# Expert blocks' token rows picked on chip by one-hot products instead of stored to memory and gathered

## Chip, cores and metric

One core of one Trainium2 chip runs the whole kernel in one launch. The metric is the device time of that launch in microseconds; lower is better.

## What is computed

Two stacks of layers follow each other on 256 latent tokens of width 1024 (256 context tokens take part in the first mixer only). The first stack has two layers, each a mixer (latent attention, then a short convolution) and a hierarchical mixture of experts. The second stack has two layers of feed-forward, attention with retention, and feed-forward again. The change touches the two mixtures of experts alone:

```
g_sel  = argmax(softmax(h @ w_group) + b_group)          # 1 of 4 groups
e_prob = softmax(logits of the 8 experts of that group)
top_w, expert_id = the 2 best of them, weights normalised, times the group's probability
for each token and each of its 2 experts e:
    y += top_w * ((silu(x @ w_gate[e]) * (x @ w_up[e])) @ w_down[e])
```

There are 32 experts of three matrices of 1024 x 512 floats (2 MB each). Everything is f32.

## The kernel before, in words

The class Moe holds an expert stage; it is used twice. `pe`, `act`, `dve` and `pool` write the program of each engine by hand, and semaphores tie them together; the order on every engine's queue is the order of the code. Tokens lie features first: A and XT hold 8 tiles of 128 features by 512 tokens. After the first mixer the context half of XT (columns 256 to 511) is not read again.

**Start of a stage.** TensorE computes the router's logits (L1495), turns the normalised tokens into rows (L1503), and runs filler products (L344, `keep_busy`). VectorE selects the experts in a long row of short steps. TensorE counts, with a triangular matrix, each token's rank within its expert (L1511). An expert's tokens are cut into blocks of CAP = 32; VectorE derives block (BLK, L1803) and place within the block (RANK) of each of the two choices of each token. One-hot matrices of place and block, multiplied (L1525), give a table that has for each block and place the token's number and weight. Meanwhile ScalarE copies the token rows out of PSUM (L1633) and stores them to the DRAM tensor f_rows (L1636). When the store has landed and the table is kept (L1821), POOL gathers the 32 rows of block 0 into XG by an indirect DMA (L1874).

**A block.** In a loop over experts, and within it over the expert's blocks (bounds read from FIRSTI):

- TensorE: gate and up products (L1573, four column groups of the array side by side), then `turn_block` (L1545: eight transposes of the gathered rows of the next block into bank 3), `combine` of the previous block's result (L1538), transposes of the hidden rows (L1589), down products (L1598).
- ScalarE: Silu (L1661), `keep_tokens` (L1652, bank 3 to XB), copy of the result (L1667), and the load of the down matrix two experts ahead (L1676).
- VectorE: Silu times up (L1833), copies of the turned hidden rows (L1839), COMBINE, the matrix that scatters the block's rows back to their tokens (L1843).
- POOL: the gather two blocks ahead (L1880, L1874).
- SP: gate and up matrices four experts ahead (L3002), issued when the expert's last L1573 is done. Ten matrices are loaded ahead of the stage: slots of the ring, three slots in the arena and A.

SP's loop of loads begins after table_kept. The lines of the change are L1393 to L1411 (semaphores), L1447 to L1460 (tiles), L1522 to L1558 and L1576 to L1578 (TensorE), L1628 to L1655 and L1663 (ScalarE), L1805 to L1843 (VectorE), L1861 to L1900 (POOL) and L2990 (SP).

## Time and profile before

| | |
|---|---|
| runs | 2455.12, 2461.4, 2458.9 us, median 2458.9 |
| span of the profiled execution | 2451.3 us |
| TensorE busy | 2077.8 us (85%), weight loads 1590.7 (65%) |
| VectorE, ScalarE, POOL busy | 1134.3 (46%), 796.4 (32%), 109.6 us (4%) |
| bytes moved | 668.86 MB, mean 273 GB/s; queue q0 (gathers) 4.20 MB |
| blocks (executions of L1833) | 70: 36 in the first expert stage, 34 in the second |

No time of the profiled execution outside of its span is shown; the span stands 7.6 us below the median of the runs, and holds all the work between the first and the last instruction. In the timeline a row is start, duration, engine, line, operation, output <- input, shapes, count, and in brackets the idle time before and what ended it. In a view by windows the columns are the stretch and its length, then busy us and instruction count of TensorE products, TensorE weight loads, VectorE, ScalarE and POOL, then the mean granted TensorE clock (1.00 is 2.4 GHz, 0.50 is 1.2 GHz), the DMA engines' busy share, and GB/s. A group of instructions has its busy time and the mean ns of one, then the idle time before them and what ended it.

### The profile page before, as it was taken

The numbers are of one execution on the slowest core, as the hardware profiler recorded it, in microseconds if no ns is written. First come the engines' busy times: TensorE is split into PE (matmuls) and PEld (weight loads), VectorE is DVE, ScalarE is ACT, GpSimd is POOL, SyncE is SP. The second block draws the span as 40 slices with busy tenths as digits, with TensorE's granted clock in tenths as the row PEclk, the third lists the DMA queues.
The fourth block names the chain that finished last, engine by engine and source line by source line (L and its number), as shares of the span: only waits on it lengthen the run. The fifth ranks groups of instructions, "written<-read, shape, count | busy, mean of one in ns | idle before, by whom it ended". The sixth has DMA issues, their size and how long they took to land.

```text
span 2451.3 us, 46085 instructions
## 1 busy us (share of the span) xinstructions
PE 2077.8 (85%) x17112; PEld 1590.7 (65%) x17113; DVE 1134.3 (46%) x2111; ACT 796.4 (32%) x1534; POOL 109.6 (4%) x188
## 2 busy tenths in 40 slices
PE   7999778666768988655557999998999999998997
PEld 3567455434446955433334788886888788886886
DVE  4677211111115641111111666776666766867666
ACT  2233101000004420000000554554554554554554
POOL 0000100000000000000000000000000000000001
PEclk9999888888879988988888999999999999999999
DMA  9875899999997569999998755325546456334552
GB/s 391 325 287 190 329 414 421 414 424 429 419 376 282 192 257 409 424 428 421 422 422 360 274 185 171 137 93 172 172 153 209 153 160 193 132 117 142 173 157 83
DMA packets 277458, 668.86 MB, mean 273 GB/s; under 512 B 8656, under 2 KB 203216, under 8 KB 252240
## 3 DMA queue, kind: packets, MB, share of 16 engines
q1 hardware_dynamic: 264416, 532.99, 57.9%
q10 hardware_dynamic: 9360, 129.96, 12.6%
q0 software_dynamic: 3552, 4.20, 0.5%
q8 instruction: 78, 1.28, 0.2%
q14 instruction: 52, 0.43, 0.1%
HBM read 669.48 MB, written 3.15 MB: 274 GB/s over the span
## 4 chain that ended last, share of the span: by engine, by line
PE 70%; DMA 14%; another core or an unknown queue 6%; DVE 5%; issue 3%; ACT 2%; SPq 1%; POOL 0%; POOLq 0%; ACTq 0%; DVEq 0%; PEldq 0%
PE ps L2180 19%; PE ps L2185 10%; PE ps L1573 9%; DMA A<-in_moe_w_up 6%; PE ps L1598 4%; DMA ring<-in_moe_w_up 4%; PE ps L2454 4%; DMA arena<-f_rows,arena 3%; PE ps L1538 2%; PE ps L1545 2%; PE ps L2619 2%; PE ps L1983 1%; PE ps L1985 1%; PE ps L1984 1%
## 5 line engine op out<-in xcount | busy, mean ns | idle before, releaser
L2180 PE MATMUL ps<-XS,WS 128*128 128x512 f32 x1408 | 499.7, 399 | 8.9 <-DVE XS L689 7.8
L2165 DVE TENSOR_TENSOR WS<-ring,WS 128x1024 fp32r<-128x1024 f32 (+1 forms) x276 | 329.5, 1195 | 226.2 <-ACT WS L2160 225.8
L2185 PE MATMUL ps<-XS,WS 128*128 128x256 f32 x1408 | 396.7, 282 | 0.0
L2160 ACT CAST WS<-ring 128x1024 fp32r<-128x1024 f32 (+1 forms) x276 | 283.0, 1026 | 328.3 <-PE ps L2185 315.0
L1833 DVE TENSOR_TENSOR arena<-arena,ps 64x256 f32<-64x256 f32 x70 | 29.6, 424 | 706.8 <-ACT arena L1661 706.8
L2180 PEld LDWEIGHTS ps<-XS,WS 128*128 128x128 f32 x1408 | 265.4, 188 | 79.3 <-DVE XS L689 18.5
L2185 PEld LDWEIGHTS ps<-XS,WS 128*128 128x128 f32 x1408 | 268.0, 190 | 0.2 <-issue 0.2
L1573 PE MATMUL ps<-arena 128*32 128x256 f32 x1632 | 159.1, 460 | 109.4 <-DMA arena<-in_moe_w_up 74.3
L1573 PE MATMUL ps<-ring,arena 128*32 128x256 f32 x2240 | 160.6, 450 | 101.3 <-DMA ring<-in_moe_w_up 93.4
L2180 PE MATMUL ps<-HS,WS 128*128 128x512 f32 x616 | 216.4, 396 | 0.0
L1598 PE MATMUL ps<-ring,arena 128*32 128x256 f32 x2240 | 165.3, 445 | 54.8 <-DVE arena L1839 54.8
L1573 PEld LDWEIGHTS ps<-ring,arena 128*32 128x32 f32 x2240 | 94.6, 129 | 168.7 <-issue 146.8
L1573 PEld LDWEIGHTS ps<-arena 128*32 128x32 f32 x1632 | 90.5, 132 | 174.5 <-issue 151.8
L2185 PE MATMUL ps<-HS,WS 128*128 128x256 f32 x704 | 197.7, 281 | 0.0
L1661 ACT ACTIVATE arena<-ps 64x256 f32<-64x256 f32 x70 | 26.3, 376 | 501.0 <-PE ps L1573 501.0
L1598 PEld LDWEIGHTS ps<-ring,arena 128*32 128x32 f32 x2240 | 88.6, 125 | 102.3 <-issue 84.0
L2185 PEld LDWEIGHTS ps<-HS,WS 128*128 128x128 f32 x704 | 133.4, 189 | 0.1
L2180 PEld LDWEIGHTS ps<-HS,WS 128*128 128x128 f32 x616 | 115.5, 188 | 26.8
L1667 ACT COPY arena<-ps 128x256 f32<-128x256 f32 x70 | 26.1, 372 | 290.8 <-PE ps L1598 290.8
L1545 PEld LDWEIGHTS ps<-BASE,arena 32*128 32x128 f32 x576 | 68.7, 198 | 56.7 <-issue 51.3
L2454 PE MATMUL ps<-XS,WS 128*128 128x256 f32 x768 | 100.4, 288 | 0.0
L1839 DVE COPY arena<-ps 64x128 f32<-64x128 f32 x140 | 39.7, 284 | 129.2 <-PE ps L1589 127.0
(352 smaller groups left out, 3212.4 us busy)
## 6 DMA issues: line engine op xcount, KB each, us to landing
ring<-in_moe_w_down ACTq DMA_DIRECT2D x60, 2048.0 KB, 14.4
ring<-in_ffn_w_gu SPq DMA_DIRECT2D x90, 1024.0 KB, 7.3
ring<-in_moe_w_gate SPq DMA_DIRECT2D x32, 2048.0 KB, 44.3
ring<-in_moe_w_up SPq DMA_DIRECT2D x32, 2048.0 KB, 52.4
arena<-in_moe_w_gate SPq DMA_DIRECT2D x32, 2048.0 KB, 44.3
ring<-in_w_mod SPq DMA_DIRECT2D x24, 2048.0 KB, 11.7
ring<-in_ffn_w_down SPq DMA_DIRECT2D x32, 1408.0 KB, 6.4
arena<-in_moe_w_up SPq DMA_DIRECT2D x16, 2048.0 KB, 53.0
```

Source lines behind the costliest of these rows:

```text
L1538: mm = pe.matmul(self.combined_tile(2 * q + i), self.YS[rows, i * P:(i + 1) * P], self.COMBINE[rows, :], start=False, stop=last and i == 1)
L1545: mm = pe.transpose(ps[:, 3, c * CAP:(c + 1) * CAP], by_eight[:, c, :], IDENT[0:CAP, 0:CAP])
L1573: mm = pe.matmul(ps[self.lane_rows(q), 0, 0:HALF_FF], x, weight, start=k == 0, stop=k == KD - 1)
L1598: mm = pe.matmul(ps[self.lane_rows(q), 7, 0:D // 4], self.HB[:, c, :], down[:, c, q * (D // 4):(q + 1) * (D // 4)], start=c == 0, stop=c = ...
L1833: v.tensor_tensor(self.H[0:2 * CAP], self.SG[2 * CAP:P], ps[2 * CAP:P, 0, 0:HALF_FF], ALU.mult)\
L1839: v.tensor_copy(self.HB[h * 2 * CAP:(h + 1) * 2 * CAP], turned[:, h]).then_inc(self.h_kept.sem, 1)
L2160: L.inc(L.eng.copy(self.parts(u)[0], source), self.w_high)
L2165: L.inc(L.eng.tensor_tensor(wl, self.unit(u)[1], high(wh), ALU.subtract), self.w_split)
L2180: L.eng.matmul(ps[:, bank, :].rearrange("p (j t) -> p j t", j=2), wh[:, i, :], moving[:, :, k, :], start=k == 0, stop=False)
L2185: mm = L.eng.matmul(ps[:, bank, 0:TL], wl[:, i, :], moving[:, 0, k, :], start=False, stop=k == total - 1)
L2454: mm = pe.matmul(out_ap, weights[:, k, :], XS[:, x, k, :], start=k == 0 and x == 0 and weights is high_part, stop=k == KD - 1 and weights ...
L2619: mm = pe.matmul(self.y_tile(m), weights[:, k - first, cols], YS[:, k, x, :], start=m % 2 == 0 and k == 0 and x == 0 and weights is high_part,
```

## The change

The rows stay on chip: ScalarE copies them into the context half of XT (ROWS). The store, f_rows, the gathers, XG, the index table and the turns of the gathered rows go. VectorE makes for each block a one-hot matrix PICK of 128 tokens by 32 places for each of the two token tiles (match: is AT, the token's block times 32 plus place less 32 for each block gone by, equal to 0..31; pick_matched adds the two choices; shift takes 32 off). TensorE multiplies with the rows as the stationary operand and PICK as the moving one (pick_block): 8 column tiles by 2 token tiles, accumulated, which gives the block's tokens features first, as the turns did. The first pick_block now stands before the zero products and the table; the table moves from bank 6 to bank 7, the fillers behind the zero products go, and the block loops and SP wait for `ranges` (FIRSTI) instead of the table.

```diff
-                self.rows_out = [shared(f"moe_rows_out{i}", 16 * NT // 2) for i in range(2)]
-                self.block_turned = sig(f"moe{l}_block_turned")
+                self.picks = sig(f"moe{l}_picks")
+                self.matched = sig(f"moe{l}_matched")
+                self.shifted = sig(f"moe{l}_shifted")
+                self.picked = sig(f"moe{l}_picked")
...
-                self.XG = take(D)
+                self.AT = take(2 * NT)
+                self.MATCH = take(2 * NT * CAP).rearrange("p (c t a) -> p c t a", c=2, t=NT)
+                self.PICK = take(NT * CAP).rearrange("p (t a) -> p t a", t=NT)
...
-                self.ROWS = [arena[:, rows_at + i * D:rows_at + (i + 1) * D] for i in range(2)]
+                self.ROWS = [XT[:, 4 * t:4 * t + 4, TL:TA] for t in range(NT)]
...
+                def pick_block():
+
+                    for c in range(KD):
+                        for t in range(NT):
+                            mm = pe.matmul(ps[:, 3, c * CAP:(c + 1) * CAP], self.ROWS[t][:, c // 2, c % 2 * P:(c % 2 + 1) * P],
+                                           self.PICK[:, t, :], start=t == 0, stop=t == NT - 1)
+                    mm.then_inc(self.picked.sem, 1)
+
+                zeros = self.YS.bitcast(BF16)
+                L.wait(self.rows_kept, NT)
+                pe.wait_ge(self.picks.sem, 1)
+                pick_block()
+                pe.wait_ge(self.y_kept.sem, 1)
+                for bank in (1, 4, 5, 6):
+                    pe.matmul(ps[:, bank, :], zeros[:, 0:P], zeros[:, 0:512], start=True, stop=False)
...
-                def turn_block():
-                    for c in range(KD):
-                        mm = pe.transpose(ps[:, 3, c * CAP:(c + 1) * CAP], by_eight[:, c, :], IDENT[0:CAP, 0:CAP])
-                    mm.then_inc(self.block_turned.sem, 1)
...
-                keep_busy(L, 7, 7)
-                pe.wait_ge(self.gathered.sem, 16)
-                turn_block()
...
-                        pe.wait_ge(self.gathered.sem, b * 16 + 32)
+                        pe.wait_ge(self.picks.sem, b + 2)
                         pe.sem_inc(spare.sem, 1)
-                        turn_block()
+                        pick_block()
...
-                    L.inc(act.copy(self.ROWS[t % 2], ps[:, 1 + 2 * (t % 2):3 + 2 * (t % 2), :].rearrange("p b n -> p (b n)")),
-                          self.rows_kept)
-                    L.join()
-                    act.dma_start(f_rows[t * P:(t + 1) * P, :], self.ROWS[t % 2]).then_inc(self.rows_out[t % 2].sem, 16)
+                    for q in range(4):
+                        rows = ps[:, 1 + 2 * t:3 + 2 * t, :].rearrange("p b n -> p (b n)").rearrange("p (n c) -> p c n", c=KD)
+                        L.inc(act.copy(self.ROWS[t][:, q, :].rearrange("p (i n) -> p i n", i=2), rows[:, 2 * q:2 * q + 2, :]),
+                              self.rows_kept if q == 3 else None)
...
+                step(v.scalar_tensor_tensor(out=self.AT, in0=self.BLK, scalar=float(CAP), in1=self.RANK, op0=ALU.mult, op1=ALU.add))
+
+                def match():
+
+                    return v.tensor_tensor(self.MATCH.rearrange("p c t a -> p (c t) a"),
+                                           IOTA[:, 0:CAP].unsqueeze(1).to_broadcast([P, 2 * NT, CAP]),
+                                           self.AT.unsqueeze(2).to_broadcast([P, 2 * NT, CAP]), ALU.is_equal)
+
+                def shift():
+                    return v.tensor_scalar(self.AT, self.AT, -float(CAP), None, ALU.add)
+
+                def pick_matched():
+                    return v.tensor_tensor(self.PICK, self.MATCH[:, 0], self.MATCH[:, 1], ALU.add)
+
+                step(match())
+                pick_matched().then_inc(self.picks.sem, 1)
+                L.inc(shift())
+                L.inc(v.tensor_copy(self.FIRSTI, self.FIRST), self.ranges)
...
+                        v.wait_ge(self.shifted.sem, b + 1)
+                        match().then_inc(self.matched.sem, 1)
+                        v.wait_ge(self.picked.sem, b + 2)
+                        v.sem_inc(spare.sem, 1)
+                        v.wait_ge(self.matched.sem, b + 1)
+                        pick_matched().then_inc(self.picks.sem, 1)
+                        shift().then_inc(self.shifted.sem, 1)
...
-                g.memset(self.XG, 0.0).then_inc(self.index_g.sem, 1)
                 g.memset(self.COMBINE, 0.0).then_inc(self.combine_made.sem, 1)
-                L.wait(self.table_kept, 1)
...
-                sp.wait_ge(moe.table_kept.sem, moe.table_kept.base + 1)
+                sp.wait_ge(moe.ranges.sem, moe.ranges.base + 1)
```

## Rows read from the trace of the kernel before

**Rows 1.** The page, section 2: GB/s moved in 40 slices of the span.

```profile
GB/s 391 325 287 190 329 414 421 414 424 429 419 376 282 192 257 409 424 428 421 422 422 360 274 185 171 137 93 172 172 153 209 153 160 193 132 117 142 173 157 83
```

**Rows 2.** View by windows: engine busy us (instructions), mean PEclk, DMA share, GB/s.

```profile
285.00:760.00 475.00, 346.21 (x4416) 217.82 (x4416) 61.32 (x189) 46.13 (x118) 39.67 (x71) 0.84 0.97 402
900.00:1360.00 460.00, 303.05 (x4232) 197.09 (x4232) 54.33 (x172) 38.48 (x104) 38.56 (x69) 0.86 0.98 406
```

**Rows 3.** Groups of instructions by line, 240 to 760 us, TensorE's first products of a block.

```profile
L1573 PE MATMUL ps<-ring,arena 128*32 128x256 f32 x1152 | 89.1, 477 | 48.9 <-DMA ring<-in_moe_w_up 45.0 <-issue 3.8
```

**Rows 4.** Timeline, TensorE, one block at full clock and the next's start.

```profile
402.78 3.66 PE L1573 MATMUL ps<-ring,arena 128*32 128x256 f32 x64 [0.24 <-issue]
406.37 0.96 PE L1545 MATMUL ps<-BASE,arena 32*128 32x32 f32 x7
407.06 0.49 PE L1538 MATMUL ps<-arena 32*128 32x256 f32 x3
...
409.55 1.93 PE L1598 MATMUL ps<-ring,arena 128*32 128x256 f32 x32 [0.78 <-DVE arena L1839]
412.36 3.66 PE L1573 MATMUL ps<-ring,arena 128*32 128x256 f32 x64 [0.87 <-issue]
```

**Rows 5.** Timeline, TensorE, first L1573 and last L1598 of both expert stages.

```profile
275.74 5.48 PE L1573 MATMUL ps<-ring,arena 128*32 128x256 f32 x64 [1.60 <-issue]
...
748.31 1.93 PE L1598 MATMUL ps<-ring,arena 128*32 128x256 f32 x32 [0.78 <-DVE arena L1839]
...
900.50 3.66 PE L1573 MATMUL ps<-ring,arena 128*32 128x256 f32 x64 [0.90 <-ACT arena L1652]
...
1355.64 1.93 PE L1598 MATMUL ps<-ring,arena 128*32 128x256 f32 x32 [0.78 <-DVE arena L1839]
```

**Rows 6.** View by windows, stretches at half clock.

```profile
286.30:289.60 3.30, 3.30 (x32) 1.89 (x36) 0.46 (x2) 0.00 (x0) 0.08 (x1) 0.50 0.04 11
296.60:299.90 3.30, 3.30 (x36) 1.97 (x34) 0.36 (x1) 0.00 (x0) 0.00 (x0) 0.50 0.98 420
887.00:890.40 3.40, 3.40 (x11) 2.22 (x11) 2.47 (x14) 0.00 (x0) 0.00 (x0) 0.50 0.29 116
890.50:893.80 3.30, 3.30 (x6) 1.60 (x6) 1.09 (x2) 0.00 (x0) 2.19 (x3) 0.50 0.00 0
```

**Rows 7.** Timeline, 289 to 300.5 us, two blocks without a weight wait between.

```profile
289.64 3.69 PE L1573 MATMUL ps<-ring,arena 128*32 128x256 f32 x64
...
293.55 0.35 SPq L3002 DMA_DIRECT2D ring<-in_moe_w_gate  x1
...
296.45 3.61 PE L1598 MATMUL ps<-ring,arena 128*32 128x256 f32 x32 [0.78 <-DVE arena L1839]
...
299.76 3.77 PE L1573 MATMUL ps<-ring,arena 128*32 128x256 f32 x64
```

**Rows 8.** View by windows, a stretch with a gather and one without.

```profile
520.00:530.00 10.00, 5.33 (x76) 2.93 (x72) 0.00 (x0) 0.37 (x1) 0.00 (x0) 0.83 1.01 403
540.00:550.00 10.00, 8.41 (x96) 5.09 (x97) 1.14 (x4) 0.75 (x2) 1.04 (x2) 0.71 1.01 433
```

**Rows 9.** Timeline, POOL, the gather before the first of these stretches.

```profile
518.44 0.93 POOL L1874 DMA_INDIRECT arena<-f_rows,arena  x1 [0.85 <-POOL arena L1880]
```

**Rows 10.** Groups by line and form: 879 to 883 us, and 239.5 to 243.2 us.

```profile
L1511 PE MATMUL ps<-arena,BASE 128*128 128x32 f32 x6 | 1.5, 405 | 2.3 <-DVE arena L1763 2.3
...
L1495 PE MATMUL ps<-VECS,A 128*128 128x36 f32 x32 | 3.7, 277 | 0.0
```

**Rows 11.** Timeline, VectorE and TensorE at the start of the expert stages.

```profile
256.98 0.16 DVE L1803 TENSOR_TENSOR arena<-arena 128x4 f32<-128x4 f32 x1
257.18 0.29 DVE L1810 TENSOR_SCALAR arena<-BASE,arena 128x128 f32<-128x128 f32 x1
...
886.88 2.62 PE L1525 MATMUL ps<-arena 128*128 128x98 f32 x8 [0.60 <-DVE arena L1815]
...
889.29 1.92 PE L1555 MATMUL ps<-arena 128*128 128x512 bf16 x4
```

More of the change, by code:

```diff
@@ L252, in carver @@
             return take
-        f_rows = nc.dram_tensor("f_rows", [TL, D], F32, kind="Internal").ap()
         const_in = sig("const_in")
@@ L1569, in expert @@
                         for k in range(KD):
-                            x = self.XB[:, k, :]
+                            x = self.XB[:, k * CAP:(k + 1) * CAP]
                             for q in range(4):
@@ L1600, in expert @@
                         mm.then_inc(self.down.sem, 1)
+                L.wait(self.ranges, 1)
                 with pe.Fori(0, EXPERTS // AHEAD) as turn:
@@ L1645, in act @@
                 L.inc(act.activation(self.ES, self.ES, ACT.Exp), self.exps)
-                for t in range(2, NT):
-                    store_rows(t)
                 load_table(L, ACT.Silu)
-                L.wait(self.table_kept, 1)
                 def keep_tokens():
-                    act.copy(self.XB.rearrange("p c a -> p (c a)"), ps[:, 3, 0:8 * CAP]).then_inc(self.x_kept.sem, 1)
-                act.wait_ge(self.block_turned.sem, 1)
+                    act.copy(self.XB, ps[:, 3, 0:KD * CAP]).then_inc(self.x_kept.sem, 1)
+                act.wait_ge(self.picked.sem, 1)
                 keep_tokens()
+                L.wait(self.ranges, 1)
                 def expert(turn, a):
@@ L1688, in act @@
                     self.next_norm.act_square(L, k)
-                L.wait(self.gathered_all, 1)
                 end(L, "act")
@@ L1816, in dve @@
                                               PLACE[:, 2, t:t + 1], ALU.is_equal, ALU.mult), self.places)
-                step(v.tensor_copy(self.FIRSTI, self.FIRST))
-                L.wait(self.table, 1)
-                tab = ps[:, 6, 0:2 * NB].rearrange("p (c b) -> p c b", c=2)
-                step(v.tensor_scalar(self.EMPTY, tab[:, 1, :], 0.5, OUT_OF_BOUNDS, ALU.is_lt, ALU.mult))
-                step(v.scalar_tensor_tensor(out=self.TABI, in0=tab[:, 1, :], scalar=-1.0, in1=self.EMPTY, op0=ALU.add, op1=ALU.add),
-                     self.table_kept)
-                step(v.tensor_copy(self.TAB, tab), self.table_kept)
                 for t in range(NT):
@@ L1826, in dve @@
                 L.join()
+                step(match())
+                v.wait_ge(self.picked.sem, 1)
+                pick_matched().then_inc(self.picks.sem, 1)
+                shift().then_inc(self.shifted.sem, 1)
+                L.wait(self.table, 1)
+                tab = ps[:, 7, 0:2 * NB].rearrange("p (c b) -> p c b", c=2)
+                step(v.tensor_copy(self.TAB, tab), self.table_kept)
                 def expert(turn, a):
@@ L1866, in pool @@
                 g.memset(self.YS, 0.0).then_inc(self.y_kept.sem, 1)
-                for i in range(2):
-                    L.wait(self.rows_out[i], 16 * (NT // 2))
-                g.memset(self.XG, 0.0).then_inc(self.index_g.sem, 1)
                 g.memset(self.COMBINE, 0.0).then_inc(self.combine_made.sem, 1)
-                L.wait(self.table_kept, 1)
-                def load_rows(indices):
-                    g.indirect_dma_start(out=self.XG[0:CAP], out_offset=None, in_=f_rows,
-                                         in_offset=bass.IndirectOffsetOnAxis(ap=indices, axis=0),
-                                         bounds_check=self.T - 1, oob_is_err=False).then_inc(self.gathered.sem, 16)
-                def gather(block, indices):
-                    g.tensor_copy(self.IDXG[0:CAP], self.TABI[0:CAP, block]).then_inc(self.index_g.sem, 1)
-                    g.wait_ge(self.index_g.sem, indices + 1)
-                    g.sem_inc(spare.sem, 1)
-                    load_rows(self.IDXG[0:CAP])
-                g.wait_ge(self.index_g.sem, 1)
-                load_rows(self.TABI[0:CAP, 0:1])
-                blocks = self.count_of(g)
-                g.wait_ge(self.gathered.sem, 16)
-                g.wait_ge(self.block_turned.sem, 1)
-                gather(slice(1, 2), 1)
-                with g.Fori(0, blocks) as b:
-                    g.wait_ge(self.gathered.sem, b * 16 + 32)
-                    g.wait_ge(self.block_turned.sem, b + 2)
-                    g.sem_inc(spare.sem, 1)
-                    gather(bass.ds(b + 2, 1), b + 2)
-                g.wait_ge(self.gathered.sem, blocks * 16 + 32)
-                g.sem_inc(self.gathered_all.sem, 1)
         take = carver()
```

31 lines of the change are left out of this document (8 added, 23 removed).

## The prediction, made before the changed kernel ran

> **What bounds the kernel now.** The page comes first. Its row of bytes moved, 40 slices of 61.3 us, shows where memory takes over: from about 310 to 670 us and from about 920 to 1290 us the DMA engines move 409 to 429 GB/s [rows 1]. These are the two expert stages, which stream 192 weight matrices of 2 MB once each. The view by windows confirms it: DMA share 0.97 to 0.98 over each stage while TensorE is busy 346 of 475 us and 303 of 460 us [rows 2]. The view of groups by line, cut to the first stage, says what TensorE waits for: 45.0 us for the expert weights in the ring slots alone to land ahead of L1573, in a group that holds a little over half of its matmuls [rows 3]. So the weight stream sets the pace in steady state, and TensorE has slack. How much slack is the question, since the change takes work from DMA and gives work to TensorE.
>
> The timeline of one undisturbed block answers that [rows 4]. L1573 starts at 402.78, the eight turns of L1545 at 406.37, the combination L1538 at 407.06, the turns of the hidden rows (L1589) follow, L1598 starts at 409.55 and lasts 1.93, and the next L1573 starts at 412.36: 9.58 us a block. There are 36 blocks in the first stage and 34 in the second (one L1833 each, counted in the table above) for 32 experts each. The first stage's blocks run from 275.74 to 748.31 + 1.93 = 750.24, the second's from 900.50 to 1355.64 + 1.93 = 1357.57 [rows 5]. That is 474.5 and 457.1 us, so 13.2 and 13.4 us a block: 3.6 to 3.9 us above 9.58 at full clock.
>
> Not all of this is waiting. Between the end of L1573 and the start of L1598, TensorE does only thin work for 3.2 us: turns of 32 rows, a combination with 32 rows, a pause of 0.78 us for VectorE. In blocks that follow each other without a weight wait, the granted clock is then 0.50, level 1.2 GHz, right behind this thin stretch (286.3 to 289.6, 296.6 to 299.9) [rows 6]. L1598 takes 3.61 instead of 1.93 us, but the next L1573 starts at once, where after a fast L1598 it starts 0.87 us late; the period is 299.76 - 289.64 = 10.12 us [rows 7].
>
> **The change, part by part.**
>
> *Removed from DMA.* Two stores of 512 KB and a gather for each block in each stage. Gathers cost more than their bytes: the stretch from 520 to 530 us runs at 403 GB/s, the one from 540 to 550 us at 433 [rows 8]; the first holds the rows of the gather issued at 518.44 [rows 9]. Half of such stretches at 7% less is 3.5% of 440 us, some 15 us a stage, if the weights stay the bound. It is worth nothing if TensorE becomes the bound, and I find below that it does.
>
> *Removed from TensorE.* Eight turns a block; the next group starts 407.06 - 406.37 = 0.69 us after them [rows 4]. The fillers of L344 at the start go too.
>
> *Added to TensorE.* pick_block: 8 column groups times 2 token tiles are 16 products. L1511 is the same form (128x128 stationary, 32 moving, f32): 3 products show as 6 instructions, so 32 instructions a block. At full clock 32 of L1495, with 36 moving columns, fill 3.7 us with a mean of 277 ns, so they start (3.7 - 0.28) / 31 = 0.11 us apart: 3.5 us. At half clock six of L1511 take 1.5 us with a mean of 405 ns, (1.5 - 0.405) / 5 = 0.22 apart: 7.0 us [rows 10]. The time is that of loading 128 columns to stream 32. No cover: it stands between L1573 and L1538, and TensorE works in order. VectorE's and ScalarE's part (Silu, product) needs 0.8 us there and was already covered.
>
> The block at full clock is therefore 9.58 - 0.69 + 3.5 = 12.4 us, 36 of them 446 us.
>
> *What the clock does to it.* The thin stretch grows from 3.2 to 3.2 - 0.69 + 3.5 = 6.0 us. Is pick_block work of the kind behind which the clock falls, or of the kind of L1573, behind which it is back? From 887.0 to 890.4 TensorE is busy without a gap (3.40 of 3.40 us), most of it with L1525: products with a 128x128 stationary operand whose loads take most of the time, as pick_block's are. The clock is 0.50 there and still 0.50 from 890.5 to 893.8 [rows 6]. TensorE had no gap and the clock did not rise. So I put pick_block with the thin work. One fall a block costs what rows 7 show: L1598 +1.7, the re-issue gap -1.07 (0.87, and 0.20 of overlap), sum 12.4 + 0.6 = 13.1 us (the same arithmetic gives 10.2 before, 10.12 seen). A stretch that is nearly twice as long holds a second fall, of some 3.3 us like those shown: it lies on pick_block or the next L1573 and costs half of itself, less what falls on the pause: 1.3 us, so 14.4 us. I take two falls in three blocks of five, 13.9 us. Below, nothing falls: 12.4. Above, all at half clock: 6.8 + 7.0 + 2 + 1.3 + 3.6 = 20.7 us, which I take as far off, since L1573 brought full clock back each time [rows 6, 7].
>
> The Trainium skill, page "TensorE: Matmul & The Clock Gate", section "HAM oscillation — how this bites in real kernels", gives as its rule that the clock is lost to idle gaps of TensorE, above all to waits for DMA. By that rule the change, which puts work where no gap is and shortens the weight waits, would keep the clock up: a block of 12.4 us and the time of rival B. The stretch from 887.0 to 890.4 [rows 6] has no gap and speaks against it.
>
> *Is the weight stream then still in the way?* An expert's 6.29 MB at 433 GB/s [rows 8] are 14.5 us; 36 blocks of 13.9 us over 32 experts are 15.6 us an expert, 34 blocks 14.8. TensorE is slower in both, so the weight waits go, and the gain on DMA with them.
>
> *Added to VectorE.* Three operations a block (128, 64 and 4 elements a lane), 0.29 us for the 128 (L1810 is such a comparison), 0.16 for the 4 (L1803), something between for the 64 [rows 11]: 0.7 us in all. They stand behind COMBINE, in a loop in which VectorE waits most of the block for ScalarE. Picks for the block after next are ready some 2 us after L1589; TensorE asks for them at the end of the next L1573, over 5 us later. Nothing. Uncovered they would cost 0.7 us a block. ScalarE: eight copies of 256 elements a lane in place of two of 1024, the same elements with six more starts, against two DMA issues and their waits removed, under VectorE's selection steps. Nothing; uncovered, an estimated 1 us a stage.
>
> *The start of a stage.* Before: store, wait for it, gather, turn, L1573 at 275.74 and 900.50 [rows 5]. After: from L1803 come AT, match and pick, three more VectorE steps, ready some 1.0 us after L1803 starts: at 258.0, and in the second stage at about 886.9, when L1525 started before [rows 11]. The clock is 0.50 there in the second stage [rows 6], and I take it so in the first, where the same short steps precede. pick_block 7.0, four zero products 1.7 (L1555, 1.92 with its tail), the table 2.6 (L1525): 11.3 to 11.4 us [rows 11]. L1573 starts at 269.4 and 898.3, that is 6.3 and 2.2 us earlier. The removed L344 fillers held the clock up in the second stage; its first L1573 will now run at half clock, +1.7. SP waited for table_kept and now waits for ranges, which comes earlier, then for the first expert's L1573; POOL is left with two memsets. On the queues of SP, ScalarE and POOL nothing new waits; VectorE has new waits on picked, with only pick_matched and shift behind them in the block.
>
> *Sum.* First stage: 269.4 + 36 x 13.9 + 1.7 = 771.5 against 750.2, +21.3. Second: 898.3 + 34 x 13.9 + 1.7 = 1372.6 against 1357.6, +15.0. Together +36.3 us on a profiled span of 2451.3. The median of the three runs is 2458.9, 7.6 above this span; added there: 2495 us.
>
> **Rivals.**
>
> *A, one fall a block (13.1 us).* Ends at 742.7 and 1345.4: -7.5 and -12.2, so 2439. For it: before, one fall is all that rows 6 show. Against: the stretch is twice as long. My 13.9 is a mixture of this and the next; the side changes at 13.4 us a block (36 x 13.4 + 34 x 13.4 + 3.4 - 8.5 = 933 against 931.6).
>
> *B, the clock holds (12.4 us): faster, and bound by weights.* The weights then end the stage: 86 loads of 2.10 MB after the ten that were prefetched, at 433 GB/s [rows 8], take 417 us. SP issues the first of them when expert 0's last L1573 is done, before at 293.55 [rows 7], then near 287 in the first stage (expert 0 has two blocks there) and 904 in the second. They end near 705 and 1322, and a block of 12.4 later the stages end at 718 and 1334: -32 and -23, so 2404. For it: TensorE has fewer gaps than before, and a product is no turn. Against: 887.0 to 893.8 [rows 6].
>
> *C, two falls in every block or more (14.4 us and up).* 36 x 14.4 + 34 x 14.4 give +39 and +32: 2530; every further 1 us a block adds 70. For it: the thin stretch is nearly twice as long in every block. Against: L1573 brought the clock back each time.
>
> **How the numbers follow.** Forecast (13.3 to 14.3 us a block) 0.60, A 0.12, B 0.15, C 0.13. The range reaches from A to a little beyond C, 2438 to 2535, and leaves out B and 0.05 of C. This kernel's measurement tells about 0.3% from no change, 7.4 us. Slower by more: the forecast but for 0.06 at its lower edge, and C: 0.67. Within: 0.09, that edge and 0.03 of A, blocks of 13.3 to 13.5 us. Faster: B and the rest of A: 0.24.
>
> **What would show it.** L1573 no longer waits for DMA after the first experts. The block period is near 13.9 us. Mean PEclk in the stages falls from 0.84 and 0.86 [rows 2] to 0.7 or lower. 32 pick instructions fill 3.5 us at full clock and 7.0 at half. DMA share falls below 0.95, with q0 gone. L1573 first starts near 269 and 898. I am wrong if the clock stays at 1.00 through pick_block, or if the stages still show 420 GB/s and more.

## The result, and the profile of the changed kernel

The changed kernel takes 2519.7 us in the median of four runs (2517.3 to 2525.6). The kernel before, run beside it on the same chip, takes 2457.0 (four runs, 2454.8 to 2461.4). The ratio is 1.025, 95% interval 1.023 to 1.028: slower by 63 us. The forecast was 2495 with a range of 2438 to 2535, so side and range hold, but the loss is nearly twice the 36 us of the sum.

The page of the changed kernel, three lines of section 2 (the span in 40 slices) and the first of section 4 (the chain that ended last):

```profile
PEclk9999777877778977787777799999999999999999
DMA  9975896999976558999997565534356456424542
GB/s 392 351 268 222 353 431 249 427 431 431 390 285 263 196 221 347 406 432 431 431 432 299 181 219 153 181 118 151 134 170 196 164 171 188 151 75 151 194 144 91
...
PE 89%; DVE 5%; issue 2%; ACT 1%; DMA 1%; SPq 0%; DVEq 0%; ACTq 0%; PEldq 0%
```

Section 3 no longer lists queue q0, the gathers'. Some slices still show 431 and 432 GB/s, the best of the stream, and others fall to 249 or 285, where before nearly all stood at 414 to 429 [rows 1]: the stream is faster when it runs, and runs less of the time. PEclk shows 7 and 8 all through the expert stages. The chain has DMA for 1%.

The view by windows, over the same two stretches as [rows 2]:

```profile
285.00:760.00 475.00, 445.67 (x4898) 306.83 (x4897) 68.57 (x264) 36.94 (x99) 0.00 (x0) 0.76 0.90 379
900.00:1360.00 460.00, 430.69 (x4535) 298.21 (x4537) 80.54 (x331) 43.31 (x112) 0.56 (x2) 0.75 0.93 393
```

TensorE is busy 445.7 and 430.7 us, where it was 346.2 and 303.1, at a clock of 0.76 and 0.75 where it was 0.84 and 0.86. The DMA share fell from 0.97 and 0.98 to 0.90 and 0.93. No wait of TensorE for a DMA is left in the first stage's L1565, where L1573 waited 45.0 us before [rows 3]. TensorE now ends both stages.

One block in TensorE's timeline (L1565 gate and up, L1520 the picks, L1547 the combination, L1581 the turns of the hidden rows, L1590 down), of the kind that fills the stages:

```profile
363.39 4.22 PE L1565 MATMUL ps<-arena 128*32 128x256 f32 x64
367.54 3.76 PE L1520 MATMUL ps<-arena,XT 128*128 128x32 f32 x32
371.23 1.99 PE L1547 MATMUL ps<-arena 32*128 32x256 f32 x16
373.15 0.64 PE L1581 MATMUL ps<-BASE,arena 64*64 64x64 f32 x4
374.57 3.64 PE L1590 MATMUL ps<-ring,arena 128*32 128x256 f32 x32 [0.78 <-DVE arena L1845]
377.95 0.53 PE L1565 MATMUL ps<-arena 128*32 128x256 f32 x2
```

The period is 377.95 - 363.39 = 14.56 us, against 9.58 in [rows 4]. The picks take 3.76. The combination takes 1.99 us where [rows 4] leaves it 1.3, and down takes 3.64, its time at half clock [rows 7], where the block of [rows 4] has 1.93. The granted clock of the stretches around it:

```profile
357.70:364.50 6.80, 6.02 (x60) 3.07 (x56) 1.66 (x7) 0.37 (x1) 0.00 (x0) 0.50 1.00 429
364.60:371.30 6.70, 6.70 (x92) 5.36 (x84) 0.42 (x1) 0.38 (x1) 0.00 (x0) 1.00 1.01 433
371.40:378.10 6.70, 5.92 (x56) 3.27 (x60) 1.66 (x7) 0.31 (x1) 0.00 (x0) 0.50 1.00 430
378.30:384.90 6.60, 6.60 (x93) 5.14 (x86) 0.42 (x1) 0.72 (x2) 0.00 (x0) 1.00 1.02 437
```

The picks and all but the first us of gate and up run at level 2.4 GHz. Behind the picks the clock is at 1.2 GHz through combination, turns, the pause and down, 6.7 us without a break, and comes back during the next gate and up. The fall does not stand at the same place in every block: in 41 of the 70 the picks take 3.7 us as here, in 29 they take 3.8 to 4.4, so that a part of them runs at the lower level. Of the 36 downs of the first stage 34 run at the lower level in whole or in part, of the 34 of the second 33; before it was 13 and 6.

Where the 68.0 us between the two profiled spans (2519.3 - 2451.3) lie, from the first and last rows of the stages in the timeline:

```profile
254.33 7.01 PE L1520 MATMUL ps<-arena,XT 128*128 128x32 f32 x32 [0.71 <-DVE arena L1804]
...
264.63 1.72 PE L1565 MATMUL ps<-ring,arena 128*32 128x256 f32 x20
...
777.80 3.48 PE L1590 MATMUL ps<-ring,arena 128*32 128x256 f32 x32 [0.78 <-DVE arena L1845]
...
931.30 1.93 PE L1565 MATMUL ps<-ring,arena 128*32 128x256 f32 x32
...
1417.77 3.64 PE L1590 MATMUL ps<-ring,arena 128*32 128x256 f32 x32 [0.78 <-DVE arena L1845]
```

| part | before [rows 5] | changed | difference | forecast |
|---|---|---|---|---|
| up to the first stage's first block | 275.74 | 264.63 | -11.1 | -6.3 |
| first stage, 36 blocks | 474.5 | 781.28 - 264.63 = 516.65 | +42.1 | 771.5 - 269.4 - 474.5 = +27.6 |
| between the stages | 150.3 | 931.30 - 781.28 = 150.0 | -0.2 | -2.2 |
| second stage, 34 blocks | 457.1 | 1421.41 - 931.30 = 490.1 | +33.0 | 1372.6 - 898.3 - 457.1 = +17.2 |
| behind it | 1093.7 | 1097.9 | +4.2 | 0 |

The blocks took 14.35 and 14.41 us on average, forecast 13.9. The 4.2 us behind the second stage stand in work that the change doesn't touch; the runs below had 1093 to 1102 us there.

### The profile page after: what moved, and what is told of

It is laid out like the page before. It is cut to its first block, busy times and chain, and to the rows that moved or that the text cites. A ratio compares the mean times of both kernels' runs of the same rounds, so it can differ in the third digit from the quotient of the medians.

```text
span 2519.3 us, 49049 instructions
## 1 busy us (share of the span) xinstructions
PE 2381.4 (95%) x18812; PEld 1833.8 (73%) x18813; DVE 1169.5 (46%) x2331; ACT 797.2 (32%) x1546; POOL 25.9 (1%) x40
## 4 chain that ended last, share of the span: by engine, by line
PE 89%; DVE 5%; issue 2%; ACT 1%; DMA 1%; SPq 0%; DVEq 0%; ACTq 0%; PEldq 0%
PE ps L2161 19%; PE ps L1520 11%; PE ps L1565 11%; PE ps L2166 10%; PE ps L1590 10%; PE ps L1547 5%; PE ps L2435 4%; PE ps L2600 2%; PE ps L1581 2%; PE ps L1964 1%; PE ps L1966 1%; PE ps L1965 1%; DVE arena L1845 1%; PE ps L1102 1%; PE ps L2476 1%
## 5 line engine op out<-in xcount | busy, mean ns | idle before, releaser
L2166 PE MATMUL ps<-XS,WS 128*128 128x256 f32 x1408 | 394.8, 280 | 0.0
L1520 PEld LDWEIGHTS ps<-arena,XT 128*128 128x128 f32 x2304 | 280.8, 202 | 33.3 <-issue 33.3
L1590 PE MATMUL ps<-ring,arena 128*32 128x256 f32 x2240 | 244.1, 611 | 54.7 <-DVE arena L1845 54.7
L1520 PE MATMUL ps<-arena,XT 128*128 128x32 f32 x2304 | 289.5, 287 | 1.4 <-DVE arena L1804 1.4
L1590 PEld LDWEIGHTS ps<-ring,arena 128*32 128x32 f32 x2240 | 110.2, 165 | 149.5 <-issue 148.3
L1565 PE MATMUL ps<-arena 128*32 128x256 f32 x1632 | 144.8, 417 | 0.8 <-issue 0.8
L1565 PE MATMUL ps<-ring,arena 128*32 128x256 f32 x2240 | 137.0, 398 | 5.7 <-issue 5.7
L1547 PE MATMUL ps<-arena 32*128 32x256 f32 x1152 | 130.2, 588 | 1.5 <-ACT arena L1656 1.5
L1565 PEld LDWEIGHTS ps<-ring,arena 128*32 128x32 f32 x2240 | 83.2, 116 | 64.7 <-issue 32.1
L1565 PEld LDWEIGHTS ps<-arena 128*32 128x32 f32 x1632 | 83.8, 122 | 62.7 <-issue 28.2
## 6 DMA issues: line engine op xcount, KB each, us to landing
ring<-in_moe_w_down ACTq DMA_DIRECT2D x60, 2048.0 KB, 13.5
ring<-in_moe_w_gate SPq DMA_DIRECT2D x32, 2048.0 KB, 13.9
```

The lines of the kernel that those rows point to most:

```text
L1520: mm = pe.matmul(ps[:, 3, c * CAP:(c + 1) * CAP], self.ROWS[t][:, c // 2, c % 2 * P:(c % 2 + 1) * P], self.PICK[:, t, :], start=t == 0, st ...
L1547: mm = pe.matmul(self.combined_tile(2 * q + i), self.YS[rows, i * P:(i + 1) * P], self.COMBINE[rows, :], start=False, stop=last and i == 1)
L1565: mm = pe.matmul(ps[self.lane_rows(q), 0, 0:HALF_FF], x, weight, start=k == 0, stop=k == KD - 1)
L1590: mm = pe.matmul(ps[self.lane_rows(q), 7, 0:D // 4], self.HB[:, c, :], down[:, c, q * (D // 4):(q + 1) * (D // 4)], start=c == 0, stop=c = ...
L2166: mm = L.eng.matmul(ps[:, bank, 0:TL], wl[:, i, :], moving[:, 0, k, :], start=False, stop=k == total - 1)
```

## The experiments

Three things had to be told apart. Is it the clock, as forecast, or only that there is more work? Does the clock fall because of where and how the products stand, and can it be had back? And is the relief on DMA worth anything, here and in the kernel before? Every run was timed against the kernel before on the same chip.

### Dense products added to the picks

```diff
                                            self.PICK[:, t, :], start=t == 0, stop=t == NT - 1)
+                        if c in (2, 5):
+                            pe.matmul(ps[:, 3, 256:512], ONES, BASE[:, 0:256], start=True, stop=True)
```

> The changed kernel with two filler products more in every pick_block (128 rows stationary, 256 columns moving, into a part of the bank that nobody reads), one after the third and one after the sixth column group. They add work and remove none. By the row of L2166 (the same form, 704 instructions in 197.1 us) a product of two instructions costs 0.56 us at that row's mean clock, so two add about 1.1 us a block. Theory 1 (the clock falls on the stretch of products with short moving operands, and the second fall in a block is there because pick_block doubled that stretch): the fillers cut the stretch, one fall a block goes, a block takes 13.1 + 0.9 = 14.0 us or less instead of 14.35 to 14.41, and the mean granted clock of the stages rises from 0.76 to over 0.85; about 2490 us, or lower, to 2440, if both falls get rarer. Theory 2 (the added work costs what it is, at the clock that the stages have anyway): 70 blocks times 1.1 us more than the changed kernel, 2597 us, clock 0.76 as before.

Measured for e_fillers: 2461.5 us (10 runs), 1.002 of the kernel before (1.001 to 1.004), so 58 us faster than the changed kernel, with more work in every block. Its view by windows, and one block (L1567 gate and up, L1523 a filler, L1520 picks, L1549 the combination):

```profile
285.00:760.00 475.00, 418.00 (x5281) 319.82 (x5281) 75.60 (x288) 42.10 (x113) 0.00 (x0) 0.97 0.93 394
900.00:1360.00 460.00, 404.91 (x5142) 310.67 (x5146) 69.52 (x268) 38.03 (x102) 0.00 (x0) 0.97 0.94 399
```

```profile
360.88 3.66 PE L1567 MATMUL ps<-arena 128*32 128x256 f32 x64 [0.89 <-issue]
...
365.84 0.68 PE L1523 MATMUL ps<-BASE 128*128 128x256 f32 x2
366.35 1.42 PE L1520 MATMUL ps<-arena,XT 128*128 128x32 f32 x12
...
369.03 1.15 PE L1549 MATMUL ps<-arena 32*128 32x256 f32 x16
...
374.08 0.41 PE L1567 MATMUL ps<-arena 128*32 128x256 f32 x2 [0.81 <-issue]
```

The clock is 0.97 in both stages, and the combination is down to 1.15 us. The next block's gate and up starts at 374.08 after this one's 360.88: 13.2 us, and the median over a stage is 13.3. A filler takes 366.35 - 365.84 = 0.51 us, so the block without its two would be 12.3 us at full clock: the 12.4 of the prediction's sum. Theory 2 is out by 135 us. Theory 1 holds, but with less than it gave: its main value was 14.0 us a block and about 2490, and 2461.5 lies between that and its low end of 2440.

### The same two products ahead of the picks

```diff
+                        for _ in range(2):
+                            pe.matmul(ps[:, 3, 256:512], ONES, BASE[:, 0:256], start=True, stop=True)
                         pick_block()
```

> The changed kernel with the same two filler products as e_fillers, but both together ahead of the picks, right behind gate and up, so that all 16 picks stay in one piece. Theory 1 (what counts is the length of the piece of short products): the piece is as long as in the changed kernel, its two falls stay, and a block takes 14.4 + 0.9 = 15.3 us; 2575 to 2585 us, granted clock about 0.77. Theory 1b (what counts is how much dense work stands in the block, wherever it is): 2461 us, as e_fillers, clock 0.97. Theory 2 (work costs what it is): that fell with e_fillers; it would give 2597.

Measured for e_fillers_ahead: 2482.6 us, 1.012 (1.008 to 1.017), clock 0.90 and 0.92 in the stages. It lies between the two theories, 37 us below the changed kernel and 21 above e_fillers. Both the amount of dense work and its place matter, and neither theory alone has it. Blocks at full clock are the same 12.39 us from the first gate product to the end of down as in e_fillers; the difference is that 32 of 70 downs are slow, against 5.

### One of them in the pause

```diff
+                        if c == 3:
+                            pe.matmul(ps[:, 3, 256:512], ONES, BASE[:, 0:256], start=True, stop=True)
...
                         mm.then_inc(self.hidden_turned.sem, 1)
+                        pe.matmul(ps[:, 7, 256:512], ONES, BASE[:, 0:256], start=True, stop=True)
```

> The changed kernel with one filler product in the middle of the picks and one behind the turns of the hidden rows, where TensorE waits 0.78 us for VectorE's copies in every block. In e_fillers a block is 12.39 us and a gap of some 0.9 us to the next, each filler in it adds 0.54. Theory 1: one filler of 0.54 less on the path, a block of 12.8 us; 2461 - 70 x 0.5 = 2426 us, clock over 0.95. Rival (the fillers must stand in the picks; one there is too few): falls come back in a part of the blocks, clock 0.80 to 0.90, 2470 to 2510 us.

Measured for e_fillers_pause: 2474.7 us, 1.008 (1.005 to 1.010), clock 0.91 in both stages. The rival holds in the time; the clock stands just above its 0.80 to 0.90. Two blocks that follow each other in its timeline show both kinds (L1549 combination, L1586 the filler in the pause, L1593 down):

```profile
408.02 1.15 PE L1549 MATMUL ps<-arena 32*128 32x256 f32 x16
...
409.48 0.70 PE L1586 MATMUL ps<-BASE 128*128 128x256 f32 x2
410.33 1.93 PE L1593 MATMUL ps<-ring,arena 128*32 128x256 f32 x32 [0.15 <-DVE arena L1848]
...
422.19 2.09 PE L1549 MATMUL ps<-arena 32*128 32x256 f32 x16
```

The filler in the pause is nearly free (the wait for VectorE shrinks from 0.78 to 0.15 us) and a block without a fall is shorter than in e_fillers, 12.8 us from gate and up to gate and up in place of 13.3. But every second or third block the clock falls again: 24 of the 70 downs take more than 2.5 us, against 5 in e_fillers, and that costs more than was saved.

### The picks twice

```diff
+                    for c in range(KD):
+                        for t in range(NT):
+                            mm = pe.matmul(ps[:, 3, c * CAP:(c + 1) * CAP], self.ROWS[t][:, c // 2, c % 2 * P:(c % 2 + 1) * P],
+                                           self.PICK[:, t, :], start=t == 0, stop=t == NT - 1)
                     mm.then_inc(self.picked.sem, 1)
```

> The changed kernel with every pick_block done twice, 16 products more in a block, with the same result. Theory 1 (the clock is at its lower level behind such products): nearly all the added work runs at half clock, 7.0 us a block, 70 x 7.0 = 490 us more, 3010 us, granted clock of the stages under 0.65. Theory 2 (the mean clock stays 0.76): 3.5 / 0.76 = 4.6 us a block, 322 us more, 2842 us.

Measured for e_double_pick: 3021.7 us, 1.232 (1.227 to 1.237), 502 us more than the changed kernel, 7.2 us a block. Theory 1's 7.0 us holds, and its clock nearly: 0.66 from 340 to 680 us and 0.67 from 1260 to 1860 us, inside the stages, where under 0.65 was expected. Theory 2 is out by 180 us. The timeline shows it (L1520 the first time, L1524 the second):

```profile
406.60 3.76 PE L1520 MATMUL ps<-arena,XT 128*128 128x32 f32 x32
410.19 6.25 PE L1524 MATMUL ps<-arena,XT 128*128 128x32 f32 x32
```

The first set runs at full clock behind gate and up, the second nearly all at half. So the first set does not pay for the lower clock, but what stands behind it does.

### The operands of the pick exchanged

```diff
-                    for c in range(KD):
-                        for t in range(NT):
-                            mm = pe.matmul(ps[:, 3, c * CAP:(c + 1) * CAP], self.ROWS[t][:, c // 2, c % 2 * P:(c % 2 + 1) * P],
-                                           self.PICK[:, t, :], start=t == 0, stop=t == NT - 1)
+                    for t in range(NT):
+                        for q in range(4):
+                            mm = pe.matmul(ps[self.lane_rows(q), 3, 256:512], self.PICK[:, t, :], self.ROWS[t][:, q, :],
+                                           start=t == 0, stop=t == NT - 1)
...
+                def turn_rows():
+                    for i in range(2):
+                        mm = pe.transpose(ps[:, 3, i * P:(i + 1) * P], self.XR[:, i * P:(i + 1) * P], IDENT)
+                    mm.then_inc(self.turned.sem, 1)
...
                         combine()
+                        pe.wait_ge(self.rows_picked.sem, b + 2)
+                        pe.sem_inc(spare.sem, 1)
+                        turn_rows()
...
+                def keep_rows():
+                    act.copy(self.XR, ps[:, 3, 256:512]).then_inc(self.rows_picked.sem, 1)
```

> The changed kernel with the operands of the pick exchanged: the one-hot places stationary (128x32) and 256 columns of rows moving, four column groups of the array side by side as in gate and up, so 8 products in place of 16; then ScalarE copies the picked rows (128x256) and TensorE turns them with two transposes of 128x128 behind the combination. Gate and up is the same form, 32 products in 3.6 us at full clock, so the 8 take 0.9 us; two transposes some 0.25 us (estimate), against 3.5 us of picks. Still no store and no gather. Theory 1 (TensorE's added time and the falls of the clock that it brings are all that made the change slower): block at full clock 9.58 - 0.69 + 1.15 = 10.0 us, with one fall 10.7, which is under the weights' 14.5 us an expert, so the weights bound again, now without gathers: between 2404 us (the prediction's rival B, at 433 GB/s) and 2440. Theory 3 (absence of gathers is worth nothing, the weights come as before): 2450 to 2459, the time of the kernel before. Theory 4 (the second fall comes from something else than the length of the stretch, such as the missing waits for weights): 2480 or more.

Measured for e_rows_moving: 2384.8 us (four runs, 2383.5 to 2389.5), ratio 0.972 (0.971 to 0.974): 72 us faster than the kernel before and 135 faster than the changed one. A block (L1523 the picks, L1557 the combination, L1529 the two turns, L1604 down), windows of both stages up to where the weights are all in, and its largest wait (us in total, times, longest):

```profile
399.24 3.66 PE L1575 MATMUL ps<-arena 128*32 128x256 f32 x64 [0.91 <-issue]
402.69 1.07 PE L1523 MATMUL ps<-XT,arena 128*32 128x256 f32 x16
403.69 1.15 PE L1557 MATMUL ps<-arena 32*128 32x256 f32 x16
404.77 0.44 PE L1529 MATMUL ps<-BASE,arena 128*128 128x128 f32 x2
405.14 0.46 PE L1595 MATMUL ps<-BASE,arena 64*64 64x64 f32 x4
406.38 1.93 PE L1604 MATMUL ps<-ring,arena 128*32 128x256 f32 x32 [0.78 <-DVE arena L1867]
409.14 0.41 PE L1575 MATMUL ps<-arena 128*32 128x256 f32 x2 [0.83 <-issue]
```

```profile
285.00:690.00 405.00, 293.08 (x4263) 181.01 (x4256) 66.44 (x256) 47.62 (x128) 0.00 (x0) 0.90 1.01 431
900.00:1270.00 370.00, 260.58 (x3752) 158.81 (x3743) 58.17 (x224) 41.71 (x112) 0.00 (x0) 0.89 1.01 431
```

```profile
PE ps L1575 <- DMA ring<-in_moe_w_up: 78.6, 20, 9.2
```

The picks start 403.69 - 402.69 = 1.0 us ahead of the combination, where they took 3.7, and the turns add 0.37, where 0.25 was estimated. The period is 409.14 - 399.24 = 9.9 us; 10.0 was expected. All 70 downs take 1.93 us. The weights bound again, at 431 GB/s without a break, and the time falls 19 us below the low end of what was expected. The stages start earlier than in the prediction's rival B (262.3 in the first), and the stretch between them is 850.21 - 708.43 = 141.8 us against 150. Of these 8 us 5 are the first picks, turns, zero products and table, 5.0 us where the changed kernel takes 10.2; the other 3 stand ahead of them and were not followed up. Against the kernel before, the profiled span is 69.6 us shorter (2451.3 - 2381.7): 47 us in the blocks of the two stages, 22 in the starts. This is the version to keep.

### The kernel before without its gathers

```diff
-                with g.Fori(0, blocks) as b:
-                    ...
-                    gather(bass.ds(b + 2, 1), b + 2)
...
-                        pe.wait_ge(self.gathered.sem, b * 16 + 32)
+                        pe.wait_ge(self.gathered.sem, 32)
```

> The kernel before, in which only the first two blocks of a stage gather their rows; all later blocks turn the rows of the second again, so the gathering of 68 of the 70 blocks is left out. TensorE's work is the same. If gathers cost the weight stream more than their bytes (403 against 433 GB/s in stretches with and without one, half of the time), the weights come some 15 us earlier in each stage and the time is about 2427 us. If they cost only their bytes (128 KB a block against 6.3 MB an expert, 2 per cent of the stream), 2440 to 2445. If the weights are not what ends the stages, or gathers are free, the same as the kernel before, 2457.

Measured for e_no_gather: 2410.5 us, 0.982 (0.980 to 0.984): 46 us, more than all three expected. From the third block of a stage on the run works on the rows of the second, so only its times say something. The same stretches of its stages and of the kernel before's, in the view by windows, first of this run:

```profile
340.00:680.00 340.00, 238.69 (x3260) 153.99 (x3257) 42.08 (x134) 29.50 (x79) 0.00 (x0) 0.88 1.01 431
980.00:1260.00 280.00, 187.20 (x2444) 118.30 (x2444) 30.34 (x96) 22.08 (x59) 0.00 (x0) 0.85 1.01 431
```

then of the kernel before:

```profile
340.00:680.00 340.00, 242.19 (x3156) 152.55 (x3160) 40.07 (x127) 28.40 (x76) 27.81 (x51) 0.85 1.01 420
980.00:1260.00 280.00, 168.36 (x2381) 108.72 (x2370) 30.07 (x95) 21.30 (x57) 21.03 (x38) 0.85 1.01 424
```

The stages take 450.1 and 436.8 us in place of 474.5 and 457.1. With gathers the stream moves 420 GB/s instead of 431, and the gathered rows are in the 420: 4.20 MB over 70 blocks, 0.06 MB in 13.2 us, 4.5 GB/s. The weights get 415.5, 3.6% less, which on the 417 us that the prediction gives for a stage's 86 loads is 15 of the 24 us that the first stage gained. In the second stage they get 419.5, which is 11 of the 20 us gained.

The rest stands at the end of the stages. Ten us near the end of the first stage, in the kernel before:

```profile
727.00:737.00 10.00, 8.88 (x120) 5.34 (x111) 1.58 (x5) 1.02 (x3) 1.11 (x2) 0.85 0.29 123
```

and without the gathers:

```profile
700.00:710.00 10.00, 7.99 (x116) 4.95 (x107) 1.57 (x5) 1.12 (x3) 0.00 (x0) 0.92 1.01 433
```

In the kernel before, the stream drops to 123 GB/s at a DMA share of 0.29 before its last up matrix has landed, for which L1573 waits until 739.86; without gathers it keeps its rate nearly to the end, and L1573 has that matrix at 713.14. At 431 GB/s the bytes of those ten us would take 3, and with the 2 to 3 us up to the landing some 9 us are lost. The second stage of the kernel before ends in the same way (268 falling to 71 GB/s from 1335 to 1347 us), also some 9 us. Together that is 15 + 9 and 11 + 9 of 24 and 20 us. Both stages of e_before_filler and e_before_two, which keep all gathers, end so too; e_rows_moving, without gathers, has 3 us of it in its first stage and none in its second. Why the last matrices land so slowly beside gathers was not found.

### The kernel before with the picks' work

```diff
+                def dummy():
+                    for c in range(KD):
+                        for t in range(2):
+                            pe.matmul(ps[:, 3, c * CAP:(c + 1) * CAP], ONES, IDENT[:, 0:CAP],
+                                      start=t == 0, stop=t == 1)
...
+                        dummy()
                         turn_block()
```

> The kernel before, gathers and turns kept, with 16 products of pick_block's form (constant 128x128 stationary, 32 columns moving, into the bank that the turns then overwrite) in every block between the wait for the gather and the turns. Theory 1 (TensorE ends the stages of the changed kernel, and the relief on DMA is worth nothing there): a block has the changed kernel's work and the turns of 0.69 us, more at half clock, on top: 2520 + 70 x 0.7 to 1.0 = 2569 to 2590 us, with no weight waits ahead of L1573. Rival (the relief is worth its 30 us also in the changed kernel): 30 us more, 2600 to 2620.

Measured for e_both: 2606.4 us, 1.062 (1.060 to 1.064), 87 us above the changed kernel. By the number the rival would hold. The profile says otherwise. This run has no DMA wait ahead of L1579, its gate and up, among its waits; one wait of 1.6 us for gathered rows stands in its first block, and the largest waits of its block loop are the pause and the re-issue gap (us in total, times, longest):

```profile
PE ps L1605 <- DVE arena L1846: 54.8, 70, 0.8
...
PE ps L1579 <- issue: 7.7, 15, 1.6
```

Its blocks are 560.9 / 36 = 15.6 and 524.9 / 34 = 15.4 us: 1.2 and 1.0 us longer than the changed kernel's, together 79 us of the 88 between the profiled spans. The first stage starts at 274.67, where the changed kernel starts at 264.63: 10 us that the expectation for theory 1 left out. On average over the 70 blocks the added products take the time of the changed kernel's picks (3.84 us to the next group, against 3.87), the turns 0.69, the combination 2.05 with the last turn in it, against 1.75, and gate and up 0.12 more: 1.1 us a block where 0.7 to 1.0 was expected. So the expectation missed by 16 us through the start and the top of its price for a block, while gathers that run beside a stage that TensorE ends cost it nothing that the waits show.

### Dense products in the kernel before

```diff
                         combine()
+                        pe.matmul(ps[:, 7, 256:512], ONES, BASE[:, 0:256], start=True, stop=True)
```

> The kernel before with one filler product (0.54 us at full clock) behind the combination of every block. It tells whether the falls of the clock cost the kernel before anything. Theory 1 (in the kernel before the weights end the stages; the granted clock of 0.84 and 0.86 costs little): clock of the stages 0.95 or more, time unchanged within 10 us, 2447 to 2467 us. Rival (the falls cost it time, as they did the changed kernel): the clock's gain shows, 2420 to 2440 us.

Measured for e_before_filler: 2459.9 us, 1.002 (1.000 to 1.004), clock 0.90 and 0.87. The clock hardly rose, so the run said little of what it was made for. Still, only 2 of the 70 downs are slow, where the kernel before has 19, and the time did not fall. With one such product ahead of the turns and two behind the combination:

> The kernel before with three filler products in every block, one ahead of the turns of the picked rows and two behind the combination (in e_before_filler one behind the combination hardly raised the clock: 0.90 and 0.87 over the two stages). They add 3 x 0.54 = 1.6 us to TensorE's work of a block, at full clock. Theory 1 (the weights end the stages of the kernel before, so neither the falls of the clock nor this added work matter much): granted clock of the stages 0.95 or more, time within 15 us of the kernel before, 2447 to 2472 us, and L1573 still waits for DMA. Rival (the falls cost the kernel before time that a steady clock gives back): 2420 to 2440 us. Second rival (TensorE is near enough to the bound that 1.6 us a block show in full): 70 x 1.6 = 112 us, 2568 us.

Measured for e_before_two: 2464.7 us, 1.0015 (0.999 to 1.004), clock 0.94 and 0.93. L1573 still waits for DMA:

```profile
PE ps L1573 <- DMA ring<-in_moe_w_up: 59.9, 15, 8.4
...
PE ps L1573 <- DMA A<-in_moe_w_up: 40.6, 11, 9.4
```

1.5 us more work in each of 70 blocks, 107 us, is swallowed by waits for weights, and a clock raised by 0.07 to 0.10 gives nothing back. The kernel before is bound by its weights, as the prediction read it.

## Why the prediction was right, and where its size was off

*What bounds the kernel before.* Right: e_before_two adds work to TensorE at no cost, e_no_gather takes load off DMA and gains 46 us.

*The block at full clock, 12.4 us.* Right: e_fillers has 13.28 us with two fillers of 0.51 each.

*The picks at 3.5 us at full clock and 7.0 at half.* Right: 3.76 as the span from first start to last end, 3.65 to 3.69 to the next group, and 7.01 at the first stage's start.

*The clock falls behind pick_block as behind thin work.* Right, and tested: dense products between the picks bring the clock back to 0.97 and win 58 us. The prediction set beside this the Trainium skill, page "TensorE: Matmul & The Clock Gate", section "HAM oscillation — how this bites in real kernels", by which idle gaps lose the clock. By it the clock should have held here, and it fell to 0.76. Gaps do not tell this loop's runs apart: the changed kernel has 0.78 us of gap a block and a clock of 0.76, e_fillers has the same 0.78 and 0.89 more ahead of L1567, and 0.97.

*Two falls in three blocks of five, 13.9 us.* This is the term that was mis-sized. The price of the two falls, 14.4 us a block, was right to 0.2 us (14.56 in the block shown, 14.35 and 14.41 on average), but they came in nearly every block: 67 of 70 downs are slow. It was rival C's case. They also lie elsewhere than I put them: not one on down and a second on the picks or the next gate and up, but, in the block shown, one stretch of 6.7 us from the combination to the start of the next block. The combination, which I left at its full-clock time, pays 0.8 us of it. The mixture had no row behind it. Nothing in the block differs from one to the next once no weight wait shifts it, so a pattern found in one block was likely to repeat in all. The miss is 0.45 and 0.51 us a block: 36 x 0.45 + 34 x 0.51 = 34 us, less 1.7 us a stage that I had added for a first L1565 at half clock; it takes 4.09 us in the first stage and 3.66, full clock, in the second.

*Two slips in the price of a fall.* 12.4 and 0.6 make 13.0 us, not 13.1, and the overlap in [rows 7] is 0.30 us, not 0.20 (296.45 + 3.61 = 300.06 against 299.76). Put right, one fall gives 12.9 us, two give 14.2, the mixture 13.7, and the forecast would have been 2480. The slips brought it 15 us nearer to the measured time, which is luck.

*The signs.* Three came out: no wait for weights, the picks' 3.7 and 7.0 us, a DMA share below 0.95. The clock of the stages, 0.76 and 0.75, stayed above the 0.7 that I gave. Of the two signs of being wrong, the first came true by its words: the clock stays at 1.00 through the picks of the block shown. What falls is the thin work behind them; that the picks bring this fall is shown by e_fillers and e_rows_moving, not by where the fall stands. The second, 420 GB/s and more, is seen in stretches (429 to 437 in the block shown) but not over the stages, 379 and 393.

*The starts.* The same VectorE step (the ranks times the choices, line 1779 now, 1791 before) stands ahead of both starts and splits them. Of the changed kernel:

```profile
251.02 0.36 DVE L1779 TENSOR_TENSOR arena<-ps,arena 128x64 f32<-128x64 f32 x2
...
917.76 0.36 DVE L1779 TENSOR_TENSOR arena<-ps,arena 128x64 f32<-128x64 f32 x2
```

and of the kernel before:

```profile
254.76 0.36 DVE L1791 TENSOR_TENSOR arena<-ps,arena 128x64 f32<-128x64 f32 x2
...
883.69 0.36 DVE L1791 TENSOR_TENSOR arena<-ps,arena 128x64 f32<-128x64 f32 x2 [0.15 <-DVE arena L1779]
```

From there to the first gate and up it was 275.74 - 254.76 = 21.0 and 900.50 - 883.69 = 16.8 us, and is 264.63 - 251.02 = 13.6 and 931.30 - 917.76 = 13.5: gains of 7.4 and 3.3 where I had 6.3 and 2.2, so the part that the change touches was right to 1.1 us, both times in its favour. The picks, zero products and table take 264.63 - 254.33 = 10.3 us, not 11.4. Ahead of that step the changed kernel's profiled run was 3.7 us earlier in the first stage, and 3.0 us later, counted from the end of the first stage, in the second. That was not followed up.

*The sum.* Blocks +30.3, starts -4.8 and +2.0, behind the stages +4.2: 31.7 us, the difference between 68.0 and 36.3.

*DMA relief worth nothing.* Right for this kernel (no wait for weights is left, and none in e_both either), but in the kernel before the gathers cost 46 us in two stages and not the 15 a stage that one pair of windows gave: the slower stream makes 15 and 11 us, and the end of the stages, which no row of mine showed, 9 each. Had TensorE not become the bound, the change would have won this; e_rows_moving shows it.

*VectorE's and ScalarE's parts.* Nothing, as forecast. L1796, L1804 and L1801 take 0.28, 0.23 and 0.16 us a block and stand in a wait.

*The offset to the median.* I added 7.6 us because the profiled span of the kernel before lay that far below its runs. The changed kernel's profiled span is 0.4 us below its median, so the 68.0 us between the spans are 61 between its median and the 2458.9 from which I started (63 from the 2457.0 of the runs beside it). That alone brought the forecast 7 us nearer.

## What to carry to other kernels

When a gather is replaced by one-hot products, let the wide side stream: 128 columns loaded to stream 32 cost 3.7 us a block here, and the same pick with places stationary and rows moving cost 1.0 and two turns of 0.37, which is the difference between 2.5% slower and 2.8% faster. Work out the block at both levels of the clock, and if a stretch of thin products brings a fall in one steady block, take it for all of them. Before paying for relief on DMA, ask if DMA still ends the stage afterwards. Where TensorE's clock is what ends it, a dense product that computes nothing can be worth more than it costs, and its place matters.

## What the runs showed of the hardware

Adding work made a kernel faster: two products of 256 columns in every block, 0.51 us each, took 58 us off, as the granted clock went from 0.76 to 0.97. The place mattered: the same two ahead of the picks gave 0.90 and 0.92, and one in the picks with one in the pause 0.91.

Small indirect gathers cost a full weight stream several times their bytes. 4.20 MB are 10 us at 431 GB/s; leaving out nearly all of them saved 46. The stream ran at 420 and 424 GB/s beside them and at 431 without, and beside them the last weights of a stage landed some 9 us late, with the DMA share down to 0.29 over ten us.
